# Recurrent layer of a hybrid trunk: order of its products, who splits its weight panels, and fused pairs of operations

## What is computed

```
gate_branch, xr = split(h @ w_in)                 # each 1024 wide
xr = centred_conv(xr, conv_w, conv_b)             # 4 taps
for each direction d (the backward one on flipped tokens):
    r, i = sigmoid of block-diagonal products of xr, 8 blocks of 128
    log_a = -8 * r * softplus(-lam);  a = exp(log_a)
    u = sqrt(-expm1(2 * log_a)) * (i * xr)
    h[t] = a[t] * h[t-1] + u[t]
y = (h_forward + h_backward) * gelu(gate_branch);  out = y @ w_out
```

## Time and profile before

| | us |
|---|---|
| median of 3 runs | 3646.51 |
| lowest and highest | 3645.62, 3653.01 |
| the profiled execution | 3648.95 |
| its span, first to last instruction | 3646.3 |
| TensorE (PE) busy in the span | 3323.3 (91%) |
| VectorE (DVE) busy | 1915.9 (53%) |
| ScalarE (ACT) busy | 1115.1 (31%) |
| GpSimd (POOL) busy | 217.2 (6%) |
| mean granted clock of TensorE | 0.959 of full speed |

### The profile page before, as it was taken

One profiled execution on the slowest core, in us unless ns is written; L12 is line 12 of the kernel. 1 busy time (PEld: TensorE's weight loads), 2 busy tenths in 40 slices (PEclk: granted clock), 3 DMA queues, 4 the chain that ended last, 5 costly groups with the idle time before them and its releaser, 6 DMA issues.

```text
span 3646.3 us, 53064 instructions
## 1 busy us (share of the span) xinstructions
PE 3323.3 (91%) x20320; PEld 3018.5 (83%) x20320; DVE 1915.9 (53%) x2728; ACT 1115.1 (31%) x1734; POOL 217.2 (6%) x120
## 2 busy tenths in 40 slices
PE   7978898999989998899999688899999776899999
PEld 2556677999987775799999566799999676899999
DVE  2133346757355665585844345575754688533332
ACT  1334433211134554321111334331111455321111
POOL 0311100000000000000000310000000342000000
PEclk9989999999999998999999899899999888999999
DMA  7300014443221110253522100163522211222222
GB/s 264 104 18 16 21 35 133 133 161 121 75 71 41 41 43 15 83 187 104 179 72 70 49 23 12 47 196 107 188 80 67 56 51 40 58 75 73 77 70 80
DMA packets 421859, 304.08 MB, mean 83 GB/s; under 512 B 12019, under 2 KB 389494, under 8 KB 421622
## 3 DMA queue, kind: packets, MB, share of 16 engines
q1 hardware_dynamic: 411412, 293.23, 26.2%
q10 hardware_dynamic: 10338, 9.41, 0.8%
HBM read 298.49 MB, written 4.10 MB: 83 GB/s over the span
## 4 chain that ended last, share of the span: by engine, by line
PE 81%; DVE 6%; ACT 6%; DVEq 2%; issue 2%; ACTq 1%; DMA 1%; SPq 0%
PE psB L295 29%; PE psA L295 29%; PE psD L295 7%; PE psC L358 3%; PE psA L339 2%; PE psC L311 2%; PE psC L350 2%; PE psB L339 2%; ACT h_hi L1339 1%; PE psA L729 1%; ACT work L1336 1%; DVE work L2216 1%; PE psB L729 1%; ACTq L1338 1%; ACT work L397 1%
## 5 line engine op out<-in xcount | busy, mean ns | idle before, releaser
L1357 ACT ACTIVATE w_hi<-raw 128x1024 fp32r<-128x1024 f32 (+1 forms) x307 | 317.3, 1035 | 1160.3 <-PE psB L295 766.3
L1870 DVE TENSOR_TENSOR w_lo<-raw,w_hi 128x1024 fp32r<-128x1024 f32 (+1 forms) x307 | 365.3, 1191 | 347.6 <-ACT w_hi L1357 347.1
L295 PE MATMUL psA<-h_hi,w_hi 128*128 128x320 f32 x1616 | 384.2, 320 | 71.9 <-DVE h_lo L1941 60.3
L295 PE MATMUL psA<-h_lo,w_hi 128*128 128x320 f32 x1616 | 375.2, 314 | 0.0
L295 PE MATMUL psA<-h_hi,w_lo 128*128 128x320 f32 x1616 | 375.1, 314 | 0.0
L295 PE MATMUL psB<-h_hi,w_hi 128*128 128x320 f32 x1616 | 368.4, 309 | 0.0
L295 PE MATMUL psB<-h_lo,w_hi 128*128 128x320 f32 x1616 | 368.2, 309 | 0.0
L295 PE MATMUL psB<-h_hi,w_lo 128*128 128x320 f32 x1616 | 368.2, 309 | 0.0
L295 PEld LDWEIGHTS psA<-h_hi,w_hi 128*128 128x128 f32 x1616 | 273.5, 192 | 91.8 <-issue 43.7
L1900 DVE SCALAR_TENSOR_TENSOR work<-work,silu_c 128x1024 f32<-128x1024 f32 x252 | 312.5, 1281 | 12.4 <-issue 0.9
L295 PEld LDWEIGHTS psA<-h_lo,w_hi 128*128 128x128 f32 x1616 | 277.0, 192 | 0.0
(11 more groups left out here) (288 smaller groups left out, 5367.6 us busy)
## 6 DMA issues: line engine op xcount, KB each, us to landing
raw<-in_w_ffn_in SPq DMA_DIRECT2D x176, 512.0 KB, 4.0
work<-in_w_mod SPq DMA_DIRECT2D x144, 512.0 KB, 4.8
raw<-in_w_ffn_out SPq DMA_DIRECT2D x64, 512.0 KB, 3.9
work<-in_w_mod SPq DMA_DIRECT2D x12, 2048.0 KB, 7.9
raw<-in_w_ffn_out SPq DMA_DIRECT2D x32, 384.0 KB, 3.4
raw<-in_diff_w_in SPq DMA_DIRECT2D x24, 512.0 KB, 3.8
raw<-in_lru_w_in SPq DMA_DIRECT2D x16, 512.0 KB, 4.6
raw<-in_gqa_w_in SPq DMA_DIRECT2D x12, 512.0 KB, 3.8
```

What stands on the lines that cost most here:

```text
L295: last = nc.tensor.matmul(out[:, b, 0:half], w[slot][:, kt * cols + c0:kt * cols + c0 + P], r[:, o:o + half], start=(kt == 0 and p == 0), ...
L1357: nc.scalar.activation(w_hi[s][:, 0:n], raw[s][:, 0:n], ACT.Copy).then_inc(hi_done, 1)
L1870: nc.vector.tensor_tensor(w_lo[s_][:, 0:n], raw[s_][:, 0:n], w_hi[s_][:, 0:n].bitcast(F32), ALU.subtract).then_inc(split_done, 1)
```

## The change

The phase "lru" becomes dense: ScalarE makes the high parts and VectorE the low parts of its panels, and GpSimd no longer has any. The first two panels (xr and gate of block 0) are split during the last projection of layer 2, as the first panels of other phases are. The panels get a new order, xr(0), gate(0), xr(1), wg(0), gate(1), xr(2), wg(1) and so on; `lru_at` turns a kind and a block into the count of a semaphore. TensorE's block becomes xr(i+1), gates(i), gate(i+1), with the gate products in psB, psC, psD, psA. ScalarE's block begins with the conversion of block i+1 and ends with the GELU of block i+1; tables are asked for by explicit loads, after the last use of the one before. VectorE's block makes `convolved(i + 1)` before m. Pairs of buffers of the two directions now lie side by side, so that square, m, square root, u and the sum are one instruction each over 1288 columns (644 for the sum), in place of two; the factors 0.5 move from u into the square and m.

```diff
@@ -142,12 +142,27 @@
         else:
-            add("lru", KT, (2, 0, 1), [(KT, P), (KT, P), (4, P)])
+            add("lru", KT, (2, 0, 1), [(KT, P), (KT, P), (4, P)], True)
...
+def lru_at(kind, i, base, ahead=0):
+    if isinstance(i, int):
+        i, ahead = i + ahead, 0
+    if kind == "xr":
+        return base if isinstance(i, int) and i == 0 else i * 3 + (base + 3 * ahead - 1)
+    if kind == "gate":
+        return i * 3 + (base + 3 * ahead + 1)
+    return base + 3 * KT - 1 if isinstance(i, int) and i == KT - 1 else i * 3 + (base + 3 * ahead + 3)
+LRU_SLOT = {"xr": 2, "gate": 0, "wg": 1}
@@ -270,9 +285,9 @@
-LRU_PE = Steps(sem("lru_pe"), ["rb", "rf", "if"], 1)
+LRU_PE = Steps(sem("lru_pe"), ["rf", "if", "rb"], 1)
...
-LRU_ACT = Steps(sem("lru_act"), ["gelu", "trb", "t", "a2", "sq"], 5)
+LRU_ACT = Steps(sem("lru_act"), ["gelu", "trf", "t", "a2", "sq"], 5)
@@ -521,10 +536,8 @@
-l_tr = [c(LW), c(LW)]
-l_ti = [c(LW), c(LW)]
-l_th = [c(LW), c(LW)]
-l_a = [c(LW), c(LW)]
+l_tr2, l_ti2, l_th2, l_a2 = (c(2 * LW) for _ in range(4))
+l_tr, l_ti, l_th, l_a = ([b_[:, d * LW:(d + 1) * LW] for d in range(2)] for b_ in (l_tr2, l_ti2, l_th2, l_a2))
@@ -671,8 +684,27 @@
-panels("lru", lambda i, j: win[:, :, bass.ds(i * P + (1 - j) * D, P)] if j < 2
-       else wg[:, :, bass.ds(i, 1), :].rearrange("k g o j -> k g (o j)"), order=(1, 0, 2))
+first = phases["lru"].first
+def lru_panel(kind, i, ahead, behind):
+    s = LRU_SLOT[kind]
+    source = (wg[:, :, bass.ds(i, 1), :].rearrange("k g o j -> k g (o j)") if kind == "wg"
+              else win[:, :, bass.ds(i * P + (ahead * P + (D if kind == "xr" else 0)), P)])
+    n = 4 if kind == "wg" else KT
+    sp.wait_ge(split_done, behind)
+    sp.dma_start(raw[s][:, 0:n * P].rearrange("p (k n) -> p k n", k=n), source).then_inc(raw_in[s], 16)
+def lru_panels(i):
+    lru_panel("xr", i, 1, lru_at("xr", i, first + 1))
+    lru_panel("wg", i, 0, i * 3 + (first + 1))
+    lru_panel("gate", i, 1, lru_at("gate", i, first + 1))
+lru_panel("gate", 0, 0, first - 1)
+lru_panel("xr", 0, 0, first - 1)
+lru_panels(0)
+with sp.Fori(1, KT - 1) as i:
+    lru_panels(i)
+lru_panel("wg", KT - 1, 0, (KT - 1) * 3 + (first + 1))
@@ -1195,19 +1227,26 @@
-def block_products(i, fresh):
-    LRU_ACT.wait(pe, "trb", i - 1)
-    h_tile(psA, "lru", i, 0, fresh).then_inc(gemm_done, 1)
-    LRU_ACT.wait(pe, "t", i - 1)
-    h_tile(psB, "lru", i, 1).then_inc(gemm_done, 1)
-    slot = take_panel(pe, "lru", i, 2)
+first = phases["lru"].first + 1
+def lru_split(at):
+    pe.wait_ge(split_done, at)
+def branch(kind, i, ps):
+    lru_split(lru_at(kind, i, first, 1))
+    products(pe, ps, LRU_SLOT[kind], KT, P, 0, h_hi, h_lo, 0, T, TH).then_inc(gemm_done, 1)
+def gates(i, more):
+    lru_split(lru_at("wg", i, first))
...
-    for g, ps, name in ((2, psA, "rb"), (0, psC, "rf"), (1, psD, "if"), (3, psB, None)):
-        if g == 3:
+    for g, ps, name in ((0, psB, "rf"), (1, psC, "if"), (2, psD, "rb"), (3, psA, None)):
+        if g == 0:
...
+        if g == 3 and more:
+            LRU_XP.wait(pe, "xp", i + 1)
...
             for b in range(2):
-                last = nc.tensor.matmul(ps[:, b, 0:LW // 2], w[slot][:, g * P:(g + 1) * P],
+                last = nc.tensor.matmul(ps[:, b, 0:LW // 2], w[1][:, g * P:(g + 1) * P],
@@ -1215,9 +1254,23 @@
-block_products(0, 6)
-with pe.Fori(1, KT) as i:
-    block_products(i, None)
+def lru_block(i):
+    LRU_ACT.wait(pe, "t", i - 1)
+    branch("xr", i, psA)
+    gates(i, True)
+    LRU_ACT.wait(pe, "trf", i)
+    branch("gate", i, psB)
+lru_split(first)
+products(pe, psA, 2, KT, P, 0, h_hi, h_lo, 0, T, TH, fresh=6).then_inc(gemm_done, 1)
+lru_split(first + 1)
+products(pe, psB, 0, KT, P, 0, h_hi, h_lo, 0, T, TH).then_inc(gemm_done, 1)
+LRU_XP.wait(pe, "xp", 0)
+lru_block(0)
+with pe.Fori(1, KT - 1) as i:
+    lru_block(i)
+LRU_ACT.wait(pe, "t", KT - 2)
+gates(KT - 1, False)
@@ -1681,53 +1734,73 @@
-def lru_block(i, more):
+ph = phases["lru"]
+def lru_high(kind, i, ahead, behind):
+    s, n = LRU_SLOT[kind], (4 if kind == "wg" else KT) * P
+    act.wait_ge(raw_in[s], i * 16 + 16 * (ph.landed[s] + ahead + 1))
+    act.wait_ge(gemm_done, behind)
+    nc.scalar.activation(w_hi[s][:, 0:n], raw[s][:, 0:n], ACT.Copy).then_inc(hi_done, 1)
+def gelu_branch(i, ahead=0):
+    nc.scalar.preload_act_table_set("gelu_apprx_tanh_and_others")
+    act.wait_ge(gemm_done, lru_at("gate", i, ph.first + 1, ahead))
+    LRU_ACT.mark(nc.scalar.activation(halves(l_gelu[:, bass.ds(i * T + ahead * T, T)], TH), psB[:, :, 0:TH],
+                                      ACT.Gelu_apprx_tanh), "gelu")
+def lru_block(i, left):
...
-    nc.scalar.preload_act_table_set("gelu_apprx_tanh_and_others")
-    g_panel("lru", i, 1)
-    LRU_ACT.mark(nc.scalar.activation(halves(l_gelu[:, bass.ds(i * T, T)], TH), psB[:, :, 0:TH],
-                                      ACT.Gelu_apprx_tanh), "gelu")
-    LRU_DVE.wait(act, "u", i - 1)
-    for g, ps, dst, ready, read in ((2, psA, l_tr[1], "rb", "trb"), (0, psC, l_tr[0], "rf", None),
-                                    (1, psD, l_ti[0], "if", None), (3, psB, l_ti[1], None, "t")):
-        if ready == "if":
+    if left > 0:
+        LRU_Y.wait(act, "y", i)
+        conv_input(lru_at("xr", i, ph.first + 1, 1))
+    if left > 1:
+        lru_high("xr", i, 2, lru_at("xr", i, ph.first + 1, 1))
+    for g, ps, dst, ready, read in ((0, psB, l_tr[0], "rf", "trf"), (1, psC, l_ti[0], "if", None),
+                                    (2, psD, l_tr[1], "rb", None), (3, psA, l_ti[1], None, "t")):
+        if g == 1:
...
         else:
-            g_panel("lru", i, 2)
+            act.wait_ge(gemm_done, lru_at("wg", i, ph.first + 1))
...
+    nc.scalar.preload_act_table_set("exp_and_others")
...
-    for d in range(2):
-        last = nc.scalar.activation(l_tr[d], l_a[d], ACT.Square)
-    LRU_ACT.mark(last, "a2")
-    if more:
-        conv_input(phases["lru"].number(i + 1, 0))
+    LRU_ACT.mark(nc.scalar.activation(l_tr2, l_a2, ACT.Square, scale=0.5), "a2")
+    nc.scalar.preload_act_table_set("sqrt_and_others")
+    if left > 0:
+        lru_high("wg", i, 1, lru_at("wg", i, ph.first + 1))
...
-    for d in range(2):
-        last = nc.scalar.activation(l_tr[d], l_th[d], ACT.Sqrt)
-    LRU_ACT.mark(last, "sq")
-conv_input(phases["lru"].number(0, 0))
-with act.Fori(0, KT - 1) as i:
-    lru_block(i, True)
-lru_block(KT - 1, False)
+    LRU_ACT.mark(nc.scalar.activation(l_th2, l_th2, ACT.Sqrt), "sq")
+    if left > 0:
+        gelu_branch(i, 1)
+    if left > 1:
+        lru_high("gate", i, 2, lru_at("gate", i, ph.first + 1, 1))
+conv_input(ph.first + 1)
+lru_high("xr", 1, 0, ph.first + 1)
+lru_high("wg", 0, 0, ph.first)
+gelu_branch(0)
+lru_high("gate", 1, 0, lru_at("gate", 0, ph.first + 1))
+with act.Fori(0, KT - 2) as i:
+    lru_block(i, 2)
+lru_block(KT - 2, 1)
+lru_block(KT - 1, 0)
@@ -2217,24 +2290,30 @@
-def lru_tail(i, more):
+def lru_low(kind, i, ahead=0):
+    s_, n = LRU_SLOT[kind], (4 if kind == "wg" else KT) * P
+    dve.wait_ge(hi_done, lru_at(kind, i, phases["lru"].dense_first + 1, ahead))
+    nc.vector.tensor_tensor(w_lo[s_][:, 0:n], raw[s_][:, 0:n], w_hi[s_][:, 0:n].bitcast(F32),
+                            ALU.subtract).then_inc(split_done, 1)
+def lru_tail(i, left):
+    if left > 1:
+        lru_low("xr", i, 2)
...
+    if left > 0:
+        dve.drain()
+        convolved(i + 1)
...
-    for d in range(2):
-        last = nc.vector.scalar_tensor_tensor(l_th[d], l_tr[d], 1.0, l_th[d], ALU.add, ALU.mult)
-    LRU_DVE.mark(last, "m")
-    dve.drain()
-    if more:
-        convolved(i + 1)
+    LRU_DVE.mark(nc.vector.scalar_tensor_tensor(l_th2, l_tr2, 0.25, l_th2, ALU.add, ALU.mult), "m")
+    if left > 0:
+        lru_low("wg", i, 1)
...
-    for d in range(2):
-        last = nc.vector.scalar_tensor_tensor(l_ti[d], l_ti[d], 0.5, l_tr[d], ALU.mult, ALU.mult)
-    LRU_DVE.mark(last, "u")
+    LRU_DVE.mark(nc.vector.tensor_tensor(l_ti2, l_ti2, l_th2, ALU.mult), "u")
@@ -2247,9 +2326,7 @@
-for t0, n, g0 in ((0, NCTX, 0), (LAT0, NLAT, NCTX)):
-    nc.vector.tensor_tensor(l_th[0][:, t0:t0 + n], l_th[0][:, t0:t0 + n],
-                            l_th[1][:, t0:t0 + n], ALU.add)
+nc.vector.tensor_tensor(l_th[0], l_th[0], l_th[1], ALU.add)
@@ -2258,11 +2335,17 @@
+    if left > 1:
+        lru_low("gate", i, 2)
+lru_low("xr", 1)
+lru_low("wg", 0)
...
-with dve.Fori(0, KT - 1) as i:
-    lru_tail(i, True)
-lru_tail(KT - 1, False)
+lru_low("gate", 1)
+with dve.Fori(0, KT - 2) as i:
+    lru_tail(i, 2)
+lru_tail(KT - 2, 1)
+lru_tail(KT - 1, 0)
@@ -2303,7 +2386,7 @@
-f"in{layer}.{ch + 1}" if ch < 2 else ("diff" if layer == 0 else None), mod,
+f"in{layer}.{ch + 1}" if ch < 2 else {0: "diff", 2: "lru"}.get(layer), mod,
```

More of the change, by code:

```diff
@@ L567, in _, with panels @@
         def _(sp):
-            def panels(name, source, order=None, units=None):
+            def panels(name, source, units=None):
                 ph = phases[name]
                 def turn(g):
```

(4 more changed lines are left out.)

## The result

| | before | after |
|---|---|---|
| median, us | 3647.61 (4 runs, 3645.62 to 3653.01) | 3604.31 (4 runs, 3599.43 to 3609.12) |
| ratio | | 0.9877 [0.9864, 0.9890] |
| profiled execution / its span | 3648.95 / 3646.3 | 3609.12 / 3606.8 |
| TensorE, VectorE, ScalarE, GpSimd busy | 3323, 1916, 1115, 217 | 3318, 1878, 1133, 118 |

The ratio stands with its 95% interval. The kernel is 43.3 us faster, against 46.5 predicted; 3604.3 lies 4.3 above the predicted 3600 and inside 3590 to 3616. In the kernel after, L310 is the product (L295 before), L1249 the gate products, L2305 the product with y (L2224), L2310 m, L2316 u, L2296 a low part, L1743 a high part.

What follows compares the result with a forecast made beforehand. VectorE, slowed by GpSimd's panel splitting, made the convolution late, so TensorE waited for `y_lo`. A block of 17.45 - 0.25 + 2.36 + 1.33 + 0.3 = 21.2 us, with the edges, saves 46.5 us: 3600 us, range 3590 to 3616.

Steps and rivals of the forecast that it cites:

- no wait on `y_lo`: Recurrent layer, TensorE: its longest wait, for the convolution's last step, eight times and 51.3 us in all, would end.
- from the end of m to u: VectorE's block: waiting for the square root, 1.3 us plus 0.03 per handover, 1.33 in all.
- The term for issue: VectorE's block: issuing the new register waits adds 0.3 us, between nothing and six at 0.16.
- The end: Block 7, from the product with y to the end of `act_lo`: 17.4 us, against 17.78 before.
- The front: Before block 0: sum of squares starts 2.2 us earlier; first product with y at 2893.0 instead of 2895.98.
- The total: Whole kernel: end of `act_lo` at 3055.2 against 3101.76, 46.5 us less, everything behind unchanged; 3600 us.
- The ring through TensorE: Rival 1: this ring, or larger VectorE gaps, sets a block of 22 to 23.7 us; 3606 to 3618, chance 0.21.
- TensorE by itself: Rival 2: VectorE is quicker than worked out and TensorE sets the block; 3579 to 3594 us, chance 0.06.
- ScalarE (0.04): Rival 3: ScalarE sets the block through costlier or additional table loads; 3602 to 3608 us, chance 0.04.
- ScalarE's copies slow VectorE as GpSimd's do: Rival 4, slower: VectorE stays slow beside ScalarE's panel copies; block 31.4 us, time 3665 us, chance 0.04.
- The fifth: Rival 5: panel or wait late once per block; 24 to 26.5 us, 3620 to 3637, chance 0.03; unchanged within 0.2%, 0.02.
- The rule that each table load drains for 1.38 us more: Counter-rule for ScalarE's block: 16.9 + 3 x 1.38 = 21.0 us plus gaps, so ScalarE would set the block.

Runs made afterwards that it cites:

- unfused: Kernel after, with square, m, square root, u and the sum made per direction again, two instructions each; 3606.10 us, one execution.
- after_third: Kernel after, unchanged, run again as the neighbour of casts_act_2; median 3599.80 us, ratio to before 0.9868.
- dve_twice: Kernel after, with the low part of the xr panel made twice in VectorE's first six blocks; 3609.69 us, one execution.
- act_twice: Kernel after, with the high part of the xr panel made twice in ScalarE's first six blocks; 3606.21 us, one execution.
- split_only: Kernel before, with only the panel splitting moved from GpSimd to ScalarE and VectorE; median 3637.39 us, ratio to before 0.9969.
- casts_act: Kernel after, with casts to `y_hi` and `act_hi` moved to ScalarE, `y_lo` and `act_lo` behind wg's low part; 3596.37 us, ratio to before 0.9866.
- pool_split: Kernel after, new order and fused operations kept, but GpSimd splitting the panels again; median 3640.34 us, ratio to before 0.9975.
- casts_act_2: The casts_act kernel measured again beside after_third; median 3594.87 us, ratio to before 0.9852.

## Why the prediction was right, and where its sizes were off

**The mechanism held.** The runs bear out no wait on `y_lo`, the low part of gate as TensorE's only regular wait, m at 1.49 us, and VectorE as what sets the block, shown by adding work to it and to ScalarE. The sizes:

| term | predicted | measured |
|---|---|---|
| block | 21.2 (20.9 to 21.9) | 20.88 to 20.92 |
| fusing, per block | 0.25 | 0.3 (unfused) |
| two low parts | 2.36 | 2.35 |
| from the end of m to u | 1.33 | 1.35 (2949.88 to 2951.23) |
| issue of the new register waits | 0.3 | about 0 |
| ScalarE busy per block | 16.9 | 17.3 (34.59 over two) |
| last product of layer 2 to L2305 of block 0 | 44.5 | 42.9 |
| seven distances of L2305 | 144.8 | 141.9 |
| L2305 of block 7 to the end of `act_lo` | 17.4 | 19.6 (18.3 in after_third) |

**The term for issue** was the one mis-sized in the block. I took 0.3, between the bound of nothing and 0.9. The rows before the low parts show no gap at all (2959.93 follows `act_lo` directly), so the low bound was right: 1.5 us in the five full blocks. The two distances behind them, with low parts missing, came to 37.5 where 38.8 were forecast, 1.3 less, about half of it the same term.

**The end** is 2.2 us longer than predicted, in "the shorter square, u and sum leave 17.4". VectorE in the last block, to be set beside the earlier trace rows:
```profile
3041.45 1.57 DVE L2305 SCALAR_TENSOR_TENSOR work<-work 128x644 f32<-128x644 f32 x2
3047.65 1.50 DVE L2310 SCALAR_TENSOR_TENSOR work<-work 128x1288 f32<-128x1288 f32 x1 [4.63 <-ACT work L1781]
3050.09 2.36 DVE L1943 TENSOR_TENSOR w_lo<-raw,w_hi 128x1024 fp32r<-128x1024 f32 x2 [0.94 <-ACT w_hi L1410]
3052.37 1.49 DVE L2316 TENSOR_TENSOR work<-work 128x1288 f32<-128x1288 f32 x1
```
Block 7 has no convolution to cover the square, and its gates wait 4.09 us for GELU, which now stands behind the square root; the last tanh ends only when VectorE comes to L2305 (3041.42), where in the block of 2941.32 it had ended 1.5 us earlier. ScalarE's timeline:
```profile
3034.41 0.70 ACT L1748 ACTIVATE work<-psB 128x640 f32<-128x640 f32 x1
3036.85 0.80 ACT L1767 ACTIVATE work<-psB,lru_small 128x644 f32<-128x644 f32 x1 [1.73 <-PE psB L1249]
...
3040.62 0.80 ACT L1767 ACTIVATE work<-psA,lru_small 128x644 f32<-128x644 f32 x1
```
After that wait the gates also run mostly at 1.2 GHz: the granted clock from 3035.3 to 3039.3 is 0.57, and 1.00 behind it. What this costs, another execution of the same kernel shows, after_third. There the gates run at 2.4 GHz from the first on, after a shorter wait, and m comes 4.87 us after L2305 in place of 6.20:
```profile
3025.71 0.54 PE L1249 MATMUL psB<-y_hi,w_hi 128*128 128x322 f32 x2 [2.57 <-ACT work L1748]
...
3031.85 1.56 DVE L2305 SCALAR_TENSOR_TENSOR work<-work 128x644 f32<-128x644 f32 x2
3036.72 1.50 DVE L2310 SCALAR_TENSOR_TENSOR work<-work 128x1288 f32<-128x1288 f32 x1 [3.31 <-ACT work L1781]
```
So 1.3 of the 2.2 us are the clock, which the prediction had at nothing here. In after's profile, from L2305 to m are 6.20 us, where the kernel before had 3088.70 - 3083.98 = 4.72 (1.5 more); m to u is 4.72 against 4.58, since the table load ahead of the copies does cost a little; u to the end 8.71 against 8.48. Together 1.85 more than the old 17.78. I had named the wait for GELU in the middle blocks, but not followed it to the last one.

**The front** came 1.6 us better than worked out, and 1.2 of it are the clock. The sum of squares starts 3.04 us behind the last product, 5.23 before: the 2.2 forecast. But it then takes 1.34 us at a grant of 1.00, where it took 2.50 at 0.50, and the prediction had left that at 2.5. That was luck, and it is given back behind the layer, where the same four matmuls, after the same wait, took 1.34 before and 2.50 now:
```profile
2859.62 1.34 PE L326 MATMUL psC<-work,consts 128*128 128x320 f32 x4 [3.04 <-DVE work L1864]
...
3155.28 1.34 PE L311 MATMUL psC<-work,consts 128*128 128x320 f32 x4 [3.04 <-DVE work L1791]
...
3114.60 2.50 PE L326 MATMUL psC<-work,consts 128*128 128x320 f32 x4 [3.05 <-DVE work L1864]
```
The middle row is of the kernel before, the others of the one after.

**The total.** From the last product of layer 2 to the end of `act_lo` the layer is 253.3 - 204.5 = 48.8 us shorter, 2.3 more than predicted: 2.9 in the blocks and 1.6 at the front, less 2.2 at the end. To the next norm 47.6 of them are left; the rest goes with the sum of squares behind the layer. That the medians show 43.3 is no further loss in the layer. The code of layer 0 is the same in both kernels, but between the first two norms it took 440.4 us in the profiled execution before, and 444.2, 437.4 and 440.5 in three profiled executions of after; layer 2's mixer took 334.8 before, and 338.1, 337.1 and 334.4. Later the same kernel had medians of 3599.07 and 3599.80, 44.2 and 48.8 under before beside it. That both lie on the predicted 3600 is in part luck: the spread is several us from one group of runs to another (before: 3643.28 to 3649.87), larger than my error in the layer.

**The rivals.** The ring through TensorE (0.21) does not set the block of after; in dve_twice two blocks of 44.4 us left it further slack. TensorE by itself (0.06) does not either: it waits in every full block, 15.5 us in six waits. ScalarE (0.04) was refuted by act_twice. That ScalarE's copies slow VectorE as GpSimd's do (0.04, the slower case) is refuted by `y_lo` at 2947.64, 0.83 us with ScalarE's copy of wg (2947.58, 0.63) beside it, and by the 5.3 us of the convolution, where block 6 before had 5.2. The fifth, where a low part is late once a block and TensorE stands as before at another semaphore, did happen, but in split_only: it is what the change's order of low parts avoids. The rule that each table load drains for 1.38 us more (the Trainium skill, ScalarE: Activation LUTs, What ACT_TABLE_LOAD costs) is not borne out here: 2946.29 + 1.28 = 2947.57, and the next instruction starts at 2947.58; with 4.1 us more a block the 19.0 of casts_act would not fit.

**The parts do not add.** Moving the split alone gives 12 us, the new order and fusing without it give 9.5, and both together 43 to 49. Each alone meets the other's limit: the order keeps TensorE fed but leaves VectorE blocked 8.4 us a block; the split frees VectorE but closes a ring through the late low part. With that low part well placed, the old order gains 37 us, and the new order with m behind the convolution brings the rest.

## What to carry to other kernels

Before an engine is relieved, follow the ring in which its last product in a block releases another engine's first: where a low part (or any small producer) stands in the queue can be worth more than who makes it, and the place to look is right behind the last thing that a waiting engine needs. Add work to one engine at a time to learn who sets a loop; here 1.2 us on VectorE came through in full in every block, and 1.05 on ScalarE in one of the five full ones. An operation moved out of a loop's critical wait must be followed into the last iteration too, where the work that covered it is missing.

## What the runs showed of the hardware

GpSimd's panel copies hold up VectorE by instruction, not by bytes: a cast, a scan of 128 columns and a multiply-add of 0.4 to 0.9 us each came to 2.3 to 2.6 in the rows of pool_split. So GpSimd's 12.7 us a block cost a loosely filled VectorE at least 6.0 and a full one 8.4, and moving its 12.7 us of work to engines where it takes 3.0 and 2.7 was cheap. And the blocks in which TensorE stood longer had the lower mean grant: 0.81 to 0.88 in four blocks of the kernel before with one wait of 7.4 us each, 0.82 to 0.90 in five of split_only with some 6 us, 0.94 to 1.00 in five of after with 1.5 to 3.3, and 1.00 in casts_act_2 with up to 1.5. The same wait does not give the same clock each time, as the sums of squares show too. The block of split_only from L2231 to L2231 in the windows view:
```profile
2962.25:2989.22 26.97, 20.86 (x122) 20.34 (x122) 18.48 (x28) 16.87 (x23) 0.00 (x0) 0.82 0.18 49
```
